# Four attention layers of an fp32 transformer: the steps of each layer in another order, written out as lists

## The reference, cut to what matters

```python
def even_mixer(h, positions, w_in, w_out):
    (aq, ak, av, ag, iq, ik, iw, bq, bk, bv, bg) = split_columns(h @ w_in, EVEN_WIDTHS)
    a = dsa_attention(aq, ak, av, iq, ik, iw) * silu(ag)   # top 64 keys by an index score
    r = head_group_norm(retention(rotary(bq), rotary(bk), bv)) * silu(bg)
    return concatenate([a, r]) @ w_out

def odd_mixer(h, ...):
    (cq, ck, cv, cg, dcq, dckv, dkr, dg) = split_columns(h @ w_in, ODD_WIDTHS)
    o = causal_attention(qs, ks, [v, v])
    c = rms_norm(o[:, :, :4] - lam * o[:, :, 4:], subln) * (1.0 - lam_init) * silu(cg)
    qd = rms_norm(dcq, q_norm) @ w_uq
    kv = rms_norm(dckv, kv_norm) @ w_ukv
    m = causal_attention(q_full, k_full, kv[..., 64:]) * silu(dg)
    return concatenate([c, m]) @ w_out

# first block: x = x + rms_norm(mixer(rms_norm(x)))   (even, then odd)
# second block, layer 0 then 1:
#   o_main = nsa_attention(...)  or  moba_attention(...)       (12 heads)
#   o_mem  = memory_attention(qm, mem, w_mem_kv)               (4 heads)
#   x = layer_norm(ALPHA * x + concatenate([o_main, o_mem]) @ w_out)
#   x = layer_norm(ALPHA * x + conv_ffn(x))
```

## Time and profile before

| | us |
|---|---|
| median of 3 runs | 938.81 (937.92 to 940.52) |
| profiled execution, its own time | 938.09 |
| its span | 936.3 |
| TensorE busy | 898.3 |
| VectorE busy | 650.2 |
| ScalarE busy | 489.0 |
| GpSimd busy | 41.4 |

### The profile page before, as it was taken

How to read it: one execution, slowest core, us unless ns; L and a number is a source line. 1 busy time by engine, 2 the same in 40 slices (tenths; PEclk the granted TensorE clock), 3 DMA queues, 4 the chain that set the end, 5 groups by cost and what they waited for, 6 DMA issues and landing times.

```text
span 936.3 us, 14616 instructions
## 1 busy us (share of the span) xinstructions
PE 898.3 (96%) x5650; PEld 772.0 (82%) x5650; DVE 650.2 (69%) x1182; ACT 489.0 (52%) x890; POOL 41.4 (4%) x73
## 2 busy tenths in 40 slices
PE   8999999799998899999999999998999999999997
...
GB/s 307 302 139 166 160 135 128 136 210 180 107 187 101 265 200 72 68 46 84 197 185 187 203 197 183 187 163 238 92 161 99 128 201 221 188 189 183 183 202 45
DMA packets 45504, 155.06 MB, mean 166 GB/s; under 512 B 5404, under 2 KB 8060, under 8 KB 45436
## 3 DMA queue, kind: packets, MB, share of 16 engines
...
q10 hardware_dynamic: 4748, 12.36, 4.1%
...
HBM read 152.78 MB, written 1.34 MB: 165 GB/s over the span
## 4 chain that ended last, share of the span: by engine, by line
PE 83%; DVE 9%; ACT 5%; issue 1%; POOL 1%; DMA 0%; DVEq 0%; ACTq 0%
PE ps L2038 16%; PE ps L2053 13%; PE ps L791 7%; PE ps L2037 7%; PE ps L684 5%; PE ps L685 5%; PE ps L686 5%; PE ps L701 4%; PE ps L703 4%; PE ps L702 4%; PE ps L871 3%; PE ps L880 2%; PE ps L923 2%; DVE wlo L652 2%; PE ps L803 1%
## 5 line engine op out<-in xcount | busy, mean ns | idle before, releaser
L652 DVE TENSOR_TENSOR wlo<-raw,whi 128x1024 fp32r<-128x1024 f32 (+1 forms) x263 | 313.5, 1214 | 31.2 <-ACT whi L646 30.8
L646 ACT ACTIVATE whi<-raw 128x1024 fp32r<-128x1024 f32 (+1 forms) x263 | 271.5, 1046 | 90.8 <-DMA raw<-in_ws 35.5
L2038 PE MATMUL ps<-t,whi 128*128 128x512 f32 x640 | 221.7, 396 | 0.0
L2037 PE MATMUL ps<-t,wlo 128*128 128x256 f32 x560 | 156.2, 279 | 0.0
L684 PE MATMUL ps<-t,whi 128*128 128x256 f32 (+1 forms) x480 | 140.4, 292 | 0.3 <-ACT arena L1668 0.3
L685 PE MATMUL ps<-t,whi 128*128 128x256 f32 (+1 forms) x480 | 136.5, 284 | 0.0
L686 PE MATMUL ps<-t,wlo 128*128 128x256 f32 (+1 forms) x480 | 136.4, 284 | 0.0
L2038 PEld LDWEIGHTS ps<-t,whi 128*128 128x128 f32 x640 | 115.9, 188 | 22.5
L2037 PEld LDWEIGHTS ps<-t,wlo 128*128 128x128 f32 x560 | 105.6, 189 | 3.6
L2053 PE MATMUL ps<-whi,r 128*128 128x512 f32 x352 | 98.0, 390 | 0.0
L684 PEld LDWEIGHTS ps<-t,whi 128*128 128x128 f32 (+1 forms) x480 | 92.3, 192 | 6.3 <-issue 4.3
...
## 6 DMA issues: line engine op xcount, KB each, us to landing
raw<-in_ws SPq DMA_DIRECT2D x256, 512.0 KB, 4.1
...
x<-in_x SPq DMA_DIRECT2D x1, 1024.0 KB, 10.3
...
```

What stands on the lines that cost most here:

```text
L646: a.i.activation(whi[:, j % NSPLIT, 0:n], raw[:, j % NRAW, 0:n], ACT.Copy).then_inc(*a.sig("hi", u))
L652: d.i.tensor_tensor(wlo[:, j % NSPLIT, 0:n], raw[:, j % NRAW, 0:n], whi[:, j % NSPLIT, 0:n].bitcast(F), ALU.subtract).then_inc(*d.sig("lo" ...
L2037: p.i.matmul(ps[:, b, 0:T], wl[:, k, :], thi[:, k, :], start=False, stop=False)
L2038: mm = p.i.matmul(ps[:, b, :], wh[:, k, :], t2[:, k, :], start=k == 0, stop=k == 7)
```

## The change

All four lists are written out step by step, each in a new order; `flow`, `woven`, `turn_of`, `tile_steps`, `chunk_steps`, `finish`, `project`, `done` and `proj` are gone. The sets of steps are the same as before (119 for EVEN, 107 for ODD, 123 for NSA, 90 for MOBA), so the program issues the same instructions, apart from their order. The start and the two feed-forward blocks are untouched. Line numbers behind the lists are smaller by 26. Cut to what is spoken of:

```diff
-    EVEN = by_rows("e_av", 0) + [("T", 1, 1)] + by_rows("e_av", 1)
...
-                  (7, [[("rope", k)] for k in range(4)]), (19, flow(dsa, 2, 4)), (12, [[("ret", k)] for k in range(7)]), (22, [[("silu", "e")]]))
...
-    EVEN += project("e", 3)
+    EVEN = [
+        ("chunk", "e_av", 0, 0), ("chunk", "e_av", 1, 0), ("chunk", "e_av", 2, 0), ("T", 1, 1), ("chunk", "e_av", 3, 0), ("rt", 0, 1),
+        ("chunk", "e_av", 0, 1), ("rt", 0, 2), ("chunk", "e_av", 1, 1), ("tile", "e_idx", 0), ("chunk", "e_av", 2, 1),
+        ("chunk", "e_av", 3, 1), ("tile", "e_idx", 1), ("tile", "e_idx", 2), ("tile", "e_rot", 0), ("rt", 1, 0), ("iw",), ("rt", 1, 1),
...
+        ("tile", "e_k", 0), ("ret", 3), ("tile", "e_k", 1), ("ret", 4), ("tile", "e_k", 2), ("ret", 5), ("tile", "e_k", 3),
+        ("log", d0), ("ret", 6), ("tile", "e_ag", 0), ("tile", "e_ag", 1), ("mul", d0), ("tile", "e_ag", 2), ("log", d1),
+        ("turn", d0, 0), ("turn", d0, 1), ("log", d2), ("mul", d1), ("tile", "e_ag", 3), ("val", d0), ("turn", d1, 0), ("mul", d2),
...
+        ("chunk", "e_bg", 2, 1), ("chunk", "e_bg", 3, 0), ("chunk", "e_bg", 3, 1), ("lo", d1), ("val", d2), ("gate", "b", 0),
+        ("proj", "e", 0, 0), ("proj", "e", 0, 1), ("proj", "e", 1, 0), ("gate", "b", 1), ("fin", d2), ("mix", "e", 2), ("lo", d2),
...
-    slots += [[("uq", 0)], [("uq", 1)], [("ukv",)]]
...
-    ODD += woven(slots, (4, [[("l2",)]]), (12, flow(mla, 2, 4)), (20, flow(diff, 3, 5)), (15, [[("silu", "o")]]))
...
+        ("tile", "o_q", 2), ("tile", "o_q", 3), ("uq", 0), ("tile", "o_kr", 0), ("uq", 1), ("ukv",), ("tile", "o_dg", 0), ("log", l0),
...
+        ("val", l2), ("chunk", "o_cg", 0, 0), ("fin", l2), ("lo", l1), ("tile", "o_k", 3), ("log", x0), ("chunk", "o_cg", 0, 1),
...
+        ("log", x2), ("mul", x0), ("chunk", "o_cg", 3, 0), ("turn", x0, 0), ("chunk", "o_cg", 3, 1), ("mul", x1), ("mul", x2),
+        ("turn", x1, 0), ("val", x0), ("fin", x0), ("turn", x2, 0), ("val", x1), ("proj", "o", 0, 0), ("fin", x1), ("val", x2),
...
-        ("w1", "k", 2), ("w1load", 6), ("tile", "a_qm", 1), ("w1", "k", 3), ("w1load", 7), ("log", m0), ("w1", "v", 0),
-        ("tile", "a_q", 0), ("w1", "v", 1), ("tile", "a_q", 1), ("mul", m0), ("w1", "v", 2), ("w1", "v", 3), ("comp", 0), ("log", m1),
-        ("turn", m0, 0), ("tile", "a_q", 2), ("log", n0), ("mul", m1), ("comp", 1), ("tile", "a_q", 3), ("turn", m0, 1), ("comp", 2),
-        ("turn", m1, 0), ("turn", m1, 1), ("val", m0), ("fin", m0), ("mul", n0), ("tile", "a_q", 4), ("log", n1), ("turn", n0, 0),
...
-        ("turn", n2, 1), ("val", n0), ("proj", "a", 1, 1), ("fin", n0), ("proj", "a", 2, 0), ("turn", n3, 0), ("cmpt", 1), ("mul", n4),
-        ("turn", n3, 1), ("val", n1), ("fin", n1), ("val", n2), ("fin", n2), ("turn", n4, 0), ("log", n6), ("mul", n5),
...
-        ("val", n7), ("proj", "a", 7, 0), ("fin", n7), ("proj", "a", 6, 1), ("norm", "a", 0), ("val", n8), ("fin", n8), ("T", 7, 0),
...
+        ("tile", "a_q", 3), ("comp", 2), ("turn", m1, 0), ("val", m0), ("turn", m1, 1), ("fin", m0), ("log", n1), ("tile", "a_q", 4),
...
+        ("proj", "a", 0, 1), ("val", n0), ("turn", n3, 0), ("mul", n4), ("turn", n3, 1), ("fin", n0), ("proj", "a", 1, 1), ("cmpt", 1),
+        ("val", n1), ("proj", "a", 2, 0), ("fin", n1), ("turn", n4, 0), ("val", n2), ("fin", n2), ("log", n6), ("proj", "a", 2, 1),
...
+        ("proj", "a", 7, 0), ("fin", n7), ("norm", "a", 0), ("val", n8), ("fin", n8), ("proj", "a", 6, 1), ("T", 7, 0),
...
-    MOBA += woven(slots, *[(k, [v]) for k, v in after.items()])
...
+        ("tile", "b_qm", 1), ("log", m0), ("tile", "b_k", 0), ("mul", m0), ("tile", "b_q", 0), ("log", m1), ("tile", "b_k", 1),
```

More of the change, by code:

```diff
@@ L464, in heads8 @@
         return [group(kind, 0, evens(0, 8), 0, 8, at), group(kind, 1, evens(0, 4), 0, 4, at), group(kind, 1, evens(4, 4), 4, 4, at + 256)]
-    def turn_of(g):
-        return [("turn", g, s) for s in range(len(g.turned))]
-    def flow(gs, lag, after):
-        out = []
-        for t in range(len(gs) + after):
-            a = []
-            if 0 <= t - lag < len(gs):
-                a += turn_of(gs[t - lag])
-            if 0 <= t - after < len(gs):
-                a += [("val", gs[t - after]), ("fin", gs[t - after])] + [("lo", gs[t - after])] * gs[t - after].gated
-            if t < len(gs):
-                a.append(("log", gs[t]))
-            if 0 <= t - lag + 1 < len(gs):
-                a.append(("mul", gs[t - lag + 1]))
-            out.append(a)
-        return out
@@ L513, in _build @@
-    EVEN += [("gate", "b", 0), ("gate", "b", 1)]
-    def finish(s, following):
-        out = [("proj", s, n, 0) for n in range(4, 8)] + [("norm", s, 0)]
-        return out + [("proj", s, n, 1) for n in range(4, 7)] + [("T", following, 0), ("proj", s, 7, 1), ("norm", s, 1)]
-    def project(s, following):
-        out = []
-        for n in range(4):
-            out += [("proj", s, n, 0), ("proj", s, n, 1)]
-            out += [("mix", s, n + 1)] if n in (1, 2) else []
-        return out + finish(s, following)
@@ L572, in _build @@
-        ("turn", m1, 0), ("turn", m1, 1), ("val", m0), ("fin", m0), ("mul", n0), ("tile", "a_q", 4), ("log", n1), ("turn", n0, 0),
-        ("turn", n0, 1), ("comp", 3), ("log", n2), ("tile", "a_q", 5), ("val", m1), ("mul", n1), ("turn", n1, 0), ("mul", n2),
-        ("fin", m1), ("turn", n1, 1), ("log", n3), ("cmp",), ("turn", n2, 0), ("add_x", "a", 0), ("add_x", "a", 1), ("cmp2",),
-        ("proj", "a", 0, 0), ("log", n4), ("cmpt", 0), ("proj", "a", 1, 0), ("log", n5), ("mul", n3), ("proj", "a", 0, 1),
@@ L580, in _build @@
-        ("mul", n7), ("proj", "a", 4, 1), ("turn", n6, 1), ("val", n5), ("fin", n5), ("proj", "a", 5, 0), ("val", n6), ("mul", n8),
-        ("fin", n6), ("proj", "a", 5, 1), ("turn", n7, 0), ("turn", n7, 1), ("proj", "a", 6, 0), ("turn", n8, 0), ("turn", n8, 1),
-        ("val", n7), ("proj", "a", 7, 0), ("fin", n7), ("proj", "a", 6, 1), ("norm", "a", 0), ("val", n8), ("fin", n8), ("T", 7, 0),
+        ("tile", "a_qm", 1), ("w1load", 6), ("w1", "k", 2), ("log", m0), ("w1", "k", 3), ("w1load", 7), ("w1", "v", 0),
@@ new lines, in _build @@
+        ("fin", m1), ("turn", n1, 0), ("turn", n1, 1), ("log", n3), ("cmp",), ("turn", n2, 0), ("add_x", "a", 0), ("add_x", "a", 1),
+        ("cmp2",), ("proj", "a", 0, 0), ("log", n4), ("cmpt", 0), ("turn", n2, 1), ("proj", "a", 1, 0), ("log", n5), ("mul", n3),
+        ("proj", "a", 0, 1), ("val", n0), ("turn", n3, 0), ("mul", n4), ("turn", n3, 1), ("fin", n0), ("proj", "a", 1, 1), ("cmpt", 1),
+        ("val", n1), ("proj", "a", 2, 0), ("fin", n1), ("turn", n4, 0), ("val", n2), ("fin", n2), ("log", n6), ("proj", "a", 2, 1),
@@ new lines, in _build @@
+        ("turn", n4, 1), ("proj", "a", 3, 0), ("proj", "a", 3, 1), ("mul", n5), ("val", n3), ("fin", n3), ("mul", n6), ("turn", n5, 0),
+        ("log", n7), ("val", n4), ("turn", n5, 1), ("fin", n4), ("proj", "a", 4, 0), ("turn", n6, 0), ("log", n8), ("val", n5),
+        ("turn", n6, 1), ("mul", n7), ("fin", n5), ("proj", "a", 5, 0), ("proj", "a", 4, 1), ("mul", n8), ("turn", n7, 0), ("val", n6),
+        ("fin", n6), ("proj", "a", 5, 1), ("turn", n7, 1), ("proj", "a", 6, 0), ("turn", n8, 0), ("turn", n8, 1), ("val", n7),
```

80 lines of the change are left out of this document (40 added, 40 removed), and 7 rows, old and new, of tables (EVEN, ODD).

## The result

The changed kernel took 928.48 us (925.57 to 931.36, 4 runs) against 939.66: a ratio of 0.9884, interval 0.9858 to 0.991. Run again beside the kernel before it took 929.75 against 938.16, ratio 0.9900, interval 0.9879 to 0.9921. So it is faster by about 1%; the medians stand 11.2 us apart the first time and 8.4 the second. The profiled execution took 931.36 us (span 929.6), 6.7 less than that of before, so part of the difference between the medians is not in these two profiles.

What follows compares the result with a forecast made beforehand. TensorE, busy 96% of the span, was taken as the bound. Waits (EVEN +2.35, ODD −0.75, NSA +1.87, MOBA −0.5, short waits +1.26) gave 4.2 us, clock 1.3: 938.81 − 5.5, rounded to 933.0, range 928.0 to 939.0.

Steps and rivals of the forecast that it cites:

- the short waits: Five waits of 0.20 to 0.36 us in ODD, NSA and MOBA lose their cause: together +1.26 us.
- T(1,1): +1.12: EVEN: T(1,1) ahead of the first rows' last e_av chunk covers the turned rows' copy and subtraction, saving 1.12 us.
- iw: +2.15: EVEN: iw behind tile e_rot 0, instead of right behind its inputs, saves its wait of 2.15 us.
- rival B: New waits as long as the old ones, above 6.2 us in sum, leaving about 937 us; chance 0.22.
- The kr term (−1.15): ODD: tile o_kr between the two uq adds waits for its bank and the key's copy, costing 1.15 us.
- +0.9 for val x0: End of ODD's differential attention: val x0 ahead of turn x2 fills part of the 1.22 us wait, saving 0.9.
- The new waits at n3 and val n1: NSA: turn n3's first side costs 1.0, its second 0.78, and val n1 behind cmpt 1 costs 0.6 us.
- The norm's place: NSA's end: norm a 0 moved earlier takes VectorE's split out of the chain ahead of T(7,0), saving 1.07 us.
- +1.3: TensorE's clock: net gain of 1.3 us from half-clock stretches going at 439.2, likelier going at 285.6, and possibly coming at n3.
- rival C: Slower: half-clock stretches move into new idle places at log d2, ukv and turn n3, giving 944.8 us; chance 0.08.
- A (929.2): The clock gains 5.1 us: stretches of 285.6 and 439.2 and half of 323.2 go, none comes; chance 0.15.
- D: VectorE's splits blocked by GpSimd's closer rotations, five losing 0.9 us each, giving 936.2 us; chance 0.05.

Runs made afterwards that it cites:

- the second profile: Profile from running the changed kernel again, unaltered, with more executions: median 929.75 us against 938.16 for the kernel before.
- the layer alone: The kernel before with only ODD's list in the new order: 937.08 us against 938.91, ratio 0.9982.
- 0.8 to 1.1 by the experiment: The changed kernel with log d2 later, mul x0 ahead of log x2 and tile o_kr back ahead of uq 0: 932.09 us.
- the fitted version: The changed kernel with 46 spare identity matmuls issued inside TensorE's waits, sized to fit them: 923.91 us, ratio 0.9837.
- 0.9 by the experiment: The changed kernel with the first rows' layer norm at NSA's end back behind proj 6: 930.66 us.

## Why the prediction was right, and where it was not

**The waits, in sum: right, by luck.** 4.2 us were forecast, 4.2 measured. With the short waits put to their layers, EVEN was forecast at 2.35 and gave 0.25, ODD at −0.33 and gave 1.4, NSA at 2.43 and gave 2.6, MOBA at −0.2 and gave nothing. EVEN's miss and ODD's cancel.

**EVEN: wrong in the waits.** The profiles stand 2.4 us apart at ODD's first tiles (194.03 against 191.64), which is the forecast's 2.35, but they get there another way: 0.2 us is ahead of the chunk behind T(1,1), none is idle time behind it (8.54 against 8.49 us), and 2.1 are busy time, in which the stretch at half clock at ODD's start is 3.4 us and not 6.8. Two more profiles with the old list have 8.58 and 8.47 us idle there, two more with the new one 8.47 and 8.52. The first projection, 0.78, log d0, 0.47 for 0.5, and log d2, 1.35 for 1.2, came as worked out: a split and four masks in front of the scores, which VectorE's timeline of the second profile shows:

```profile
126.18 1.22 DVE L626 TENSOR_TENSOR wlo<-raw,whi 128x1024 fp32r<-128x1024 f32 x1
127.32 0.41 DVE L958 CUSTOM_DVE_ANT_0 sm<-ps,arena 128x256 f32<-128x256 f32 x1
```

"T(1,1): +1.12" is not to be told from this pair: 0.85 us are left in it. That wait hangs on the start of the program as well: in the nine profiles with the new list up to there it was between less than 0.15 and 1.70 us. Eight of them are at that chunk at 43.97 to 44.68 us, the ninth at 46.27, and the five with the old list at 44.88 to 46.08: 0.9 between the medians. The step that failed is "A wait that goes counts with its own row", for "iw: +2.15": the wait has gone, and 1.10 came at the retention, which I had not counted; VectorE was at 24.21 of 25 us there, and the text said so only under rival B. The last proj and T(3,0): 5.0 us of waits before, 5.3 after, near the nothing that was forecast. That a shorter or missing stretch at ODD's start belongs to the new list is likely (6.8 us in all four profiles with the old one whose waits were not filled; 0, 3.4, 3.4, 3.4, 3.4 and 6.8 with the new one), but why was not settled.

**ODD: wrong in sign.** "−0.75" was forecast; the profiles stand 1.7 us further apart behind it, and the layer alone gained 1.8. The kr term (−1.15) was right: 0.8 to 1.1 by the experiment. Log x0 was 0.57 for 0.5. The waits at the three turns were 1.03, 2.26 and 1.22 us, 4.5 in all; one of 2.39 is left. VectorE's timeline after shows what it does then:

```profile
277.00 0.20 DVE L998 RECIPROCAL stat<-stat 128x8 f32<-128x8 f32 x1
...
277.44 0.87 DVE L1004 TENSOR_SCALAR sm<-sm,stat 128x128 f32<-128x128 f32 x4
278.34 1.14 DVE L1009 SCALAR_TENSOR_TENSOR sm<-sm,stat 128x128 f32<-128x128 f32 x4
279.40 1.22 DVE L626 TENSOR_TENSOR wlo<-raw,whi 128x1024 fp32r<-128x1024 f32 x1
```

TensorE waits for the first product; the last o_cg chunk then stands between this turn and the next, and val x0 before the third, and under their cover VectorE makes the other two. In this profile the cover is complete because TensorE is at half clock from 279.2 on. At full clock 0.87 and 0.24 us are left as well, 3.5 in all with the 2.39: the order itself saved 1.0, near the +0.9 for val x0, and "the pacing itself stays" holds. The step that failed is that waits and clock were added up as if apart, at 1.7 us for a stretch wherever it stands: the one from 279.2 costs nothing, as ODD, from its tiles of the second rows to T(5,1), takes 123.05 and 123.08 us with it and 123.02 without (the fitted version). Before, ODD took 124.78 us with a stretch of 3.4 us behind the last of the three turns, where no such wait hides it. The new waits eat the 1.0, so most of the 1.7 must be there; but another profile with the old list takes 124.79 with 6.8 us at half clock there, and one without any, its waits unfilled, was not seen: this is argued and not shown.

**NSA: right, a little low.** Forecast 1.87, and 0.56 of the short waits. The rows above and one of 0.36 sum to 3.20, against 5.79 before: 2.6. The new waits at n3 and val n1 were priced at 2.38 and were 1.33: the first side of turn n3, priced at 1.0, has none, its second took 0.75 for 0.78, and val n1 0.58 for 0.6. Turn m0 brought 0.78, but 0.46 of it came back at val m0, which had no term, and mul n1 brought 0.32 for 0.55. The norm's place brought 1.23 in the row for 1.07, and 0.9 by the experiment.

**MOBA: right.** 0.47 for 0.5 came at log m0, and the short waits went, one of 0.23 that was not counted among them.

**The clock: wrong in this pair, and its spread missed.** +1.3 was forecast; in the two profiles it is 20.4 against 20.4 us at half clock. The stretch at 439.2 went, as forecast. None stands behind n3's waits (393.92 and 396.95), where one was forecast: the new one begins at 378.2, ahead of them, and the second profile does not have it. "The two of 6.8 us stand behind layer boundaries that stay" failed at both: they became 3.4 and 10.2. But over many executions the changed kernel is at 0.988 to 0.997 and the kernel before at 0.982 to 0.990. The means differ by 0.003, which is 2.8 of 930 us at most; the medians (8.4 and 11.2) differ by 1.7 and 4.5 beyond the profiles (6.7), so the clock can be the 1.7 and only part of the 4.5. The forecast rested on one execution of before, which had no stretch behind the wait of 2.15 at iw; three of the next four profiles with that order had one. I used its absence as an argument against rival C.

**The rivals.** A (929.2) is nearest in number. Its mechanism is there only in part: of its three stretches that of 439.2 went, that of 285.6 moved to where it costs nothing, and that of 323.2 grew. B is refused by the time; in its own sign it is close, as the new waits were 1.10, 0.47, 1.35, 0.6, 0.57, 1.33 and 0.47, 5.9 us, and 6.4 with the 0.46 at val m0, against the 6.2 that was to decide. That around uq and ukv was 2.2 us, as the sign had it, but its longest, 1.06, is ended by VectorE's eviction (L1682) and not by ScalarE. C is refused in its sign. D: the splits beside GpSimd's rotations took a little more than the earlier trace rows:

```profile
L626 DVE TENSOR_TENSOR wlo<-raw,whi 128x1024 fp32r<-128x1024 f32 x9 | 13.0, 1448 | 0.0
```

1448 ns for 1376, 0.65 us in nine. D and its price of 0.9 us rest on a misreading of the mean and of the 1.80: the 1.80 us are not a rotation's own length. Before, on GpSimd and on VectorE:

```profile
82.59 1.60 POOL L1540 TENSOR_TENSOR arena<-arena,tb 128x256 f32<-128x256 f32 x1
...
84.15 0.74 POOL L1541 TENSOR_TENSOR arena<-arena,tb 128x256 f32<-128x256 f32 x1
```

```profile
81.92 1.68 DVE L652 TENSOR_TENSOR wlo<-raw,whi 128x1024 fp32r<-128x1024 f32 x1
...
88.28 1.72 DVE L652 TENSOR_TENSOR wlo<-raw,whi 128x1024 fp32r<-128x1024 f32 x1
```

An instruction of the rotation takes 0.74 us. The four that begin inside a split (at 76.59, 79.22, 82.59 and 85.78) take 1.60 to 1.80, and each ends 0.6 us after the split does. The four splits that begin inside a rotation instruction (at 76.17, 81.92, 85.41 and 88.28) take 1.37 to 1.72 for 1.22, at most 0.5 more. The Trainium skill, "SBUF — State Buffer", section "SBUF: two separate sides", says that the later of the two is blocked for the other's whole instruction; these rows agree with that, for GpSimd above all. So the rule holds and the rival falls by its price: after the change the longest splits there take 1.71 us.

Left open: TensorE's busy time fell by 2.2 us with the same instructions. By layers it is 2.1 less in EVEN, 0.4 less in ODD, 2.2 more in NSA and 1.8 less behind it, as the stretches moved. 0.5 of the sum is that only 18.4 us of the stretches at half clock were filled with work, against 19.3; what the rest is was not settled.
